# Gate and up projections by seven block products, the down projection as a phase of its own, the final norm in the last block

## What is computed

```python
h = h + mixed @ w_out[l]
u = rmsnorm(h, ln2_g[l])
h = h + (jax.nn.silu(u @ w_ffn_gate[l]) * (u @ w_ffn_up[l])) @ w_ffn_down[l]
# after both layers
return rmsnorm(h, final_norm_g)
```

## Time and profile before

| | us |
|---|---|
| median of three runs | 2712.1 |
| profiled execution, its own time | 2710.6 |
| span of that execution, first to last instruction | 2708.5 |
| gate, up and down part of layer 1 (end of the output projection to the end of the down projection) | 723.8 |
| the same of layer 2 | 720.6 |
| from there to the end of the span | 31.1 |

### The profile page before, as it was taken

One profiled execution on the slowest core, in us unless ns is written; L12 is line 12 of the kernel. 1 busy time (PEld: TensorE's weight loads), 2 busy tenths in 40 slices (PEclk: granted clock), 3 DMA queues, 4 the chain that ended last, 5 costly groups with the idle time before them and its releaser, 6 DMA issues. The chain is left out here.

```text
span 2708.5 us, 32110 instructions
## 1 busy us (share of the span) xinstructions
PE 2622.1 (97%) x13272; PEld 2079.0 (77%) x13272; DVE 1265.8 (47%) x1297; ACT 681.0 (25%) x884; POOL 923.8 (34%) x416
## 2 busy tenths in 40 slices
PE   7999998999999999999999999899999999999997
PEld 5777765678888888888877777567888888888885
DVE  7877368522333333333567753964323333333334
ACT  6344156621000000000234331854110000000002
POOL 2000431155444444444520023122664444444432
PEclk9999999999999999999999999999999999999998
DMA  5010200022111111111210111002121111111102
GB/s 180 24 40 16 54 22 1 20 98 62 55 47 46 46 46 46 46 51 57 70 56 19 38 39 43 1 1 86 48 63 58 58 46 46 54 46 46 46 24 62
DMA packets 198129, 129.59 MB, mean 48 GB/s; under 512 B 29330, under 2 KB 187154, under 8 KB 198035
## 3 DMA queue, kind: packets, MB, share of 16 engines
q1 hardware_dynamic: 198034, 128.25, 15.5%
HBM read 115.65 MB, written 12.58 MB: 47 GB/s over the span
## 5 line engine op out<-in xcount | busy, mean ns | idle before, releaser
L221 PE MATMUL ps<-u_hi,w_hi 128*128 128x512 f32 x2304 | 730.3, 398 | 27.3 <-DVE f L867 13.2
L221 PE MATMUL ps<-u_hi,w_lo 128*128 128x512 f32 x2304 | 713.6, 391 | 0.0
L221 PE MATMUL ps<-u_lo,w_hi 128*128 128x512 f32 x2304 | 713.2, 391 | 0.0
L221 PEld LDWEIGHTS ps<-u_hi,w_hi 128*128 128x128 f32 x2304 | 428.6, 189 | 128.4 <-issue 25.0
L221 PEld LDWEIGHTS ps<-u_hi,w_lo 128*128 128x128 f32 x2304 | 434.5, 189 | 91.8
L221 PEld LDWEIGHTS ps<-u_lo,w_hi 128*128 128x128 f32 x2304 | 434.2, 188 | 91.7
L1820 POOL TENSOR_TENSOR w_hi<-w_raw,ones 128x1024 fp32r<-128x1024 f32 x88 | 166.7, 1894 | 417.0 <-PE ps L221 412.5
L1892 DVE TENSOR_TENSOR h<-ps,h 128x1024 f32<-128x1024 f32 x176 | 211.4, 1219 | 157.4 <-PE ps L221 157.4
L1823 POOL TENSOR_TENSOR w_lo<-w_raw,w_hi 128x1024 fp32r<-128x1024 f32 x88 | 250.7, 2849 | 6.9
L1877 DVE TENSOR_TENSOR hidden<-ps,hidden 128x1024 f32<-128x1024 f32 x44 | 53.9, 1224 | 422.1 <-PE ps L221 422.1
L204 POOL TENSOR_TENSOR w_hi<-w_raw,ones 128x1024 fp32r<-128x1024 f32 (+1 forms) x37 | 71.0, 1918 | 481.8 <-DMA w_raw<-w_in 229.6
(11 more groups left out here) (316 smaller groups left out, 2999.8 us busy)
## 6 DMA issues: line engine op xcount, KB each, us to landing
w_raw<-w_gate SPq DMA_DIRECT2D x44, 512.0 KB, 3.7
w_raw<-w_up SPq DMA_DIRECT2D x44, 512.0 KB, 3.8
down_raw<-w_down SPq DMA_DIRECT2D x44, 512.0 KB, 4.8
w_raw<-w_in SPq DMA_DIRECT2D x42, 512.0 KB, 3.9
h_spill<-h SPq DMA_DIRECT2D x16, 512.0 KB, 2.9
w_raw<-w_out SPq DMA_DIRECT2D x16, 512.0 KB, 3.9
h<-h_spill SPq DMA_DIRECT2D x16, 512.0 KB, 7.1
x_in<-x SPq DMA_DIRECT2D x8, 512.0 KB, 6.7
```

Of the source, the lines that this page charges most:

```text
L221: last = nc.tensor.matmul(ps[:, bank0 + half, :], a, b[:, half * HALF:(half + 1) * HALF], start=(k == order[0] and n == 0), stop=(k == ord ...
```

## The change

For one tile of 128 hidden features, gate and up together are a product of a 2x2 block matrix of weights (gate, up by input features 0 to 511, 512 to 1023) with a 2x2 block matrix of activations (those input features by tokens 0 to 511, 512 to 1023). The change computes it with seven block products (Strassen's scheme in Winograd's form) where eight were done. Each of the seven takes four tiles of input features, three passes and 512 tokens: 12 matmuls. P1 and P6 are accumulated in one bank, P5 and P3 in another, P7 and P4 in a third, P2 has a fourth; two sets of four banks alternate from tile to tile. The four weight sums S1 to S4 are made on VectorE for each tile, the four activation sums T1 to T4 once per layer. ScalarE takes the high parts of the seven weight blocks of a tile, POOL the low parts.

The hidden tile is no longer used at once: it is stored to DRAM (`hidden_dram`) and read back in a down phase of 11 chunks, which starts when all 22 tiles of gate and up are done. `h` is overwritten in place to make room, so it is stored to DRAM tile by tile (`h_spilled`) and loaded again ahead of the down phase. The loops of the block are written out, and setup semaphores are given back.

In the last layer the final norm is done in the same block: gains on ScalarE, transposes of the unscaled tiles, the factor per token as a column, applied by ScalarE and VectorE as they copy out of PSUM. The block `final` is gone.

```diff
+        W_ORDER = ["A11", "A12", "A22", "S3", "S1", "S2", "S4"]
+        W_ORDER0 = ["A11", "A12", "S1", "S2", "S4", "S3", "A22"]
+        S_ORDER = ["S3", "S1", "S2", "S4"]
+        PRODUCTS = dict(P1=("A11", "B11"), P2=("A12", "B21"), P3=("S4", "B22"), P4=("A22", "T4"),
+                        P5=("S1", "T1"), P6=("S2", "T2"), P7=("S3", "T3"))
+        BANK = dict(P1=0, P6=0, P5=1, P3=1, P2=2, P7=3, P4=3)
+        P_ORDER = ["P1", "P7", "P5", "P6", "P2", "P3", "P4"]
+        P_ORDER0 = ["P1", "P5", "P2", "P3", "P7", "P6", "P4"]
...
+            def load_weights(sp, i, t):
+                if i == 0:
+                    sp.wait_ge(slot_split, KT - 3 + t)
+                elif t == 0:
+                    sp.wait_ge(w_lo, 7 * i if i == 1 else 7 * (i - 1) + 3)
+                    sp.wait_ge(s_ready, 4 * i)
...
+            def store_hidden(sp, i):
+                sp.wait_ge(hid_done, i + 1)
+                sp.dma_start(hidden_dram[i * P:(i + 1) * P, :], GA[:, :]).then_inc(hid_stored, 16)
...
+            def pe_product(pe, i, name):
...
+                pe.wait_ge(w_lo, weight_at(i, a))
+                if name == "P6":
+                    pe.wait_ge(p1_copied, i + 1)
+                if name == "P3":
+                    pe.wait_ge(p5_copied, i + 1)
+                if name == "P4":
+                    pe.wait_ge(w_summed, i + 1)
...
+            def dve_c22(dve, i):
+                dve.wait_ge(p_done, product_at(i, "P7"))
+                dve.wait_ge(v_copied, i + 1)
+                nc.vector.tensor_tensor(WT[:, :], ps[:, bank(i, "P7"), :], VC[:, :], ALU.add).then_inc(w_summed, 1)
...
+                nc.vector.tensor_tensor(UP[:, HALF:S], WT[:, :], P5C[:, :], ALU.add).then_inc(up_part, 1)
...
+            def dve_c12(dve, i):
...
+                nc.vector.tensor_tensor(GA[:, HALF:S], ps[:, bank(i, "P3"), :], VC[:, :], ALU.add)\
+                    .then_inc(gate_part, 1)
...
+                nc.vector.tensor_tensor(GA[:, :], GA[:, :], RS[:, :], ALU.mult).then_inc(gate_scaled, 1)
...
+            def dve_c21(dve, i):
+                dve.wait_ge(p_done, product_at(i, "P4"))
+                nc.vector.tensor_tensor(UP[:, 0:HALF], ps[:, bank(i, "P4"), :], VC[:, :], ALU.add)\
+                    .then_inc(up_part, 1)
...
+                nc.vector.tensor_tensor(UP[:, :], UP[:, :], RS[:, :], ALU.mult).then_inc(up_scaled, 1)
...
+                nc.vector.tensor_tensor(GA[:, :], GA[:, :], UP[:, :], ALU.mult).then_inc(hid_done, 1)
...
             # SP
+                    for i in range(1, TILES):
+                        load_weights(sp, i, 0)
+                        load_weights(sp, i, 1)
+                        store_hidden(sp, i - 1)
...
             # POOL
+                    for i in range(1, TILES):
+                        for name in W_ORDER:
+                            pool_weight(pool, i, name)
...
             # ScalarE
+                    for i in range(1, TILES):
+                        act_silu(act, i - 1)
+                        act_p1(act, i)
+                        if i + 1 < TILES:
+                            for name in W_ORDER[0:4]:
+                                act_weight(act, i + 1, name)
+                        act_p5(act, i)
+                        if i + 1 < TILES:
+                            for name in W_ORDER[4:6]:
+                                act_weight(act, i + 1, name)
...
+                        act_v(act, i)
+                        if i + 1 < TILES:
+                            act_weight(act, i + 1, W_ORDER[6])
...
             # VectorE, first tile and then the others
+                    u_part("B21", 3)
+                    dve_sums(dve, 0, S_ORDER0[3:4])
+                    for k in range(4):
+                        u_part("T3 raw", k)
+                        u_part("T2 raw", k)
+                    for k in range(4):
+                        u_part("B22", k)
+                    dve_c11(dve, 0)
+                    for name in ("T4 raw", "T2", "T4"):
+                        for k in range(4):
+                            u_part(name, k)
+                    dve_sums(dve, 1, S_ORDER)
                     dve.wait_ge(rstd_ready, 1)
+                    dve_c22(dve, 0)
+                    dve_c12(dve, 0)
+                    for i in range(1, TILES):
+                        dve_c21(dve, i - 1)
+                        if i + 1 < TILES:
+                            dve_sums(dve, i + 1, S_ORDER)
+                        dve_c22(dve, i)
+                        dve_c11(dve, i)
+                        dve_c12(dve, i)
+                        if i + 1 == TILES:
+                            dve_hidden(dve, 0)
+                    dve_c21(dve, TILES - 1)
```

More of the change, by code:

```diff
@@ new lines, in build @@
+        U_HI = [("B11", 0), ("B11", 1), ("T1", 0), ("B11", 2), ("T1", 1), ("UG", 0), ("B11", 3), ("T1", 2), ("UG", 1),
+                ("B21", 0), ("T1", 3), ("UG", 2), ("B21", 1), ("UG", 3), ("B21", 2), ("B21", 3)] + \
+               [(b, k) for b in ("B22", "T3", "T2", "T4") for k in range(4)]
+        U_HI_AT = {x: n + 1 for n, x in enumerate(U_HI)}
+        U_DVE = [("B11", 0), ("T1 raw", 0), ("B11", 1), ("T1 raw", 1), ("T1", 0), ("B11", 2), ("T1 raw", 2), ("T1", 1),
+                 ("B11", 3), ("T1 raw", 3), ("T1", 2), ("B21", 0), ("T1", 3), ("B21", 1), ("B21", 2), ("B21", 3)] + \
+                [(b, k) for k in range(4) for b in ("T3 raw", "T2 raw")] + \
+                [(b, k) for b in ("B22", "T4 raw", "T2", "T4") for k in range(4)]
@@ new lines, in build @@
+        U_DVE_AT = {x: n + 1 for n, x in enumerate(U_DVE)}
+        DRAW = [raw[t] for t in range(2)]
+        DSET = [[at_r(f"down{s}_{x}{t}", 64 + 16 * s + 8 * n + 4 * t, [P, D], F32R) for n, x in enumerate(("hi", "lo"))
+                 for t in range(2)] for s in range(2)]
+        HRAW = [at_u(f"hidden_back{t}", 16 + 4 * t, [P, S]) for t in range(2)]
+        HIDH = [at_r(f"hidden_hi{b}", 16 * b, [P, 2, S], F32R) for b in range(2)]
+        HIDL = [at_r(f"hidden_lo{b}", 16 * b + 8, [P, 2, S], F32R) for b in range(2)]
@@ L2077, in _ @@
-                    act_chunk(act, 0, 0, first=True)
-                    with act.Fori(0, (CHUNKS - 1) // 2) as r:
-                        for b in range(2):
-                            act_chunk(act, 2 * r + (b + 1), (b + 1) % 2)
+                        norm_act(act, norm2, m, SQ2, None, None)
+                        at = sum(steps[:m])
+                        for name, k in U_HI[at:at + steps[m]]:
+                            u_part(name, k)
+                    for name in W_ORDER0[0:5]:
+                        act_weight(act, 0, name)
@@ new lines, in _ @@
+                    for name in ("T2", "T4"):
+                        for k in range(4):
+                            u_part(name, k)
+                    act.wait_ge(proj_done, J_OUT + KT + 1)
+                    norm_rs(act, 0, (rs_part, 1))
+                    act.wait_ge(h_spilled, 16 * KT)
+                    for name in W_ORDER[0:3]:
+                        act_weight(act, 1, name)
+                    act_v(act, 0)
+                    for name in W_ORDER[3:7]:
+                        act_weight(act, 1, name)
@@ L2090, in _ @@
+                    act.wait_ge(rstd_ready, 2)
+                    for part in range(2):
+                        for n in range(0, TT, 2):
+                            t = OUT_ORDER[n]
+                            act.wait_ge(tokens_done, TT * part + n + 1)
+                            nc.scalar.activation(OT[:, t, part * HALF:(part + 1) * HALF], ps[:, t, :], ACT.Copy,
+                                                 scale=RST[:, t:t + 1]).then_inc(out_act, 1)
                 @block.vector
@@ new lines, in _ @@
+                        if m == KT - 2:
+                            dve_sums(dve, 0, S_ORDER0[0:3])
+                            u_part("B21", 2)
+                    u_part("B21", 3)
+                    dve_sums(dve, 0, S_ORDER0[3:4])
+                    for k in range(4):
+                        u_part("T3 raw", k)
+                        u_part("T2 raw", k)
+                    for k in range(4):
+                        u_part("B22", k)
+                    dve_c11(dve, 0)
+                    for name in ("T4 raw", "T2", "T4"):
+                        for k in range(4):
+                            u_part(name, k)
@@ new lines, in _ @@
+                        return
+                    dve.wait_ge(rstd_ready, 2)
+                    for part in range(2):
+                        for n in range(1, TT, 2):
+                            t = OUT_ORDER[n]
+                            dve.wait_ge(tokens_done, TT * part + n + 1)
+                            nc.vector.tensor_tensor(OT[:, t, part * HALF:(part + 1) * HALF], ps[:, t, :],
+                                                    RST[:, t:t + 1].broadcast_to([P, HALF]), ALU.mult)\
+                                .then_inc(out_dve, 1)
```

705 lines of the change are left out of this document (460 added, 245 removed).

## The result

| | before | after |
|---|---|---|
| median of six runs each, us | 2712.0 (2710.6 to 2714.2) | 2722.6 (2721.6 to 2724.4) |
| ratio, 95% interval | | 1.0041 (1.0030 to 1.0052) |
| span of the profiled execution | 2708.5 | 2719.7 |
| feed-forward part of layer 1 / 2 | 723.8 / 720.6 | 732.7 / 730.1 |
| from there to the end of the span | 31.1 | 23.2 |

The kernel became 10.6 us slower. The forecast was 2680: the direction is wrong, though the time lies in the range. The feed-forward part after is read from the start of the first block product (632.3 and 1966.4) to the start of the last addition of the down projection (1365.0 and 2696.5).

A forecast was written before the change was run, and what follows sets the result against it. TensorE, busy 97% of the span, was taken as the bound. Per layer -59.8 + 17.2 + 3 + 22 + 4.9 + 1 + 1.6 - 1.5 = -11.6; twice that and -8.5 is -31.7, giving 2680 us, range 2628 to 2725.

The forecast's parts named there:

- the end: From the last addition to the span's end: final norm with transposes and one-column products, 8.5 us gained (4 to 11).
- Part 1: Gate and up matmuls: 84 passes per tile instead of 96 at the old pace, floor 19.04 us, 59.8 us less per layer.
- Part 3: SP's queue in gate and up: store and loads wait for the previous hidden tile; 20.24 us per tile, 22 us per layer.
- the ring: Loop per tile: hidden tile's end, store and next loads (5.9 us), VectorE's work to the next end; 20.24 us in all.
- list of signs: What a trace would show if right: P3 waits about 1.2 us for the copy of P5, period 20.2, down 24 us into tile 21.
- Part 2: Engine work per tile: VectorE 9.5 us, POOL 9, ScalarE 7, all under 19.04, but VectorE and POOL block each other.
- the hold-ups: VectorE instructions with two SBUF operands wait out a full POOL instruction, also at 512 elements: 4.7 us per tile.
- engine part: The ring from first weight sum to the hidden tile's end: 9.5 us of VectorE's own work and 4.7 of hold-ups.
- The first tile: Start of gate and up: P4 starts 34.6 us after P1, 17.2 us lost per layer, plus 3 for the clock.
- part 5: From up to down: 4.9 us lost before down, about 1 for the clock, 1.6 for reloads of h, nothing for hidden loads.
- the second rival: Gate and up: the ring is longer, from 21.1 us per tile the kernel is slower than before; chance 0.18.
- Without hold-ups 15.5: Lower bound of the ring per tile in us, if VectorE is never held up: TensorE sets the pace, 0 lost.

The follow-up runs named there:

- run 1: Against the kernel after, SP issues tile i's two weight loads ahead of the store of hidden tile i-2, so loads no longer wait for the previous hidden tile: 2644.3 us.
- run 4: Against the kernel after, GpSimd fills the low parts of gate and up weights with zero from tile 2 on, reading no operand: 2645.1 us.
- run 2: Against the kernel after, loads still wait for the previous hidden tile's end, but its store goes out behind the two loads: 2681.7 us.
- run 3: Against the kernel after, loads still wait for the previous hidden tile's end, but its store goes out from ScalarE's queue instead of SP's: 2736.0 us.
- run 5: Against the kernel after, down weights and hidden tiles of chunk 1 are issued between the fourth and fifth reloads of h, not behind all eight: 2707.7 us.

## Why the prediction was wrong

Against the sum, per layer, layer 1 / layer 2:

| step | forecast | measured |
|---|---|---|
| gate and up, first to last pass | 462.1 | 475.5 / 477.3 |
| pause ahead of down | 5.9 | 3.6 / 3.5 |
| down phase | 241.0 | 250.3 / 249.1 |
| all of it against before | -11.6 | +8.9 / +9.5 |
| the end | -8.5 | -7.9 |

The forecast of 462.1 is 22 x 19.04 + 17.2 + 3 + 22 and the 1.0 of the norm's sum.

*Right.* Part 1, the pace: 19.04 us per tile in the open ring (run 1). Part 3, the mechanism and place of the ring: P3 waits for the copy of P5, its chain runs hidden, DMA, VectorE, as the forecast's list of signs says. Part 2, the hold-ups at 512 elements: S2 1.65, gate x RS 2.26, gate x up 2.21 in the chain above, and 0.69 for S2 without POOL's subtraction (run 4). The Trainium skill ("SBUF — State Buffer", section Terms) gave that rule, and the traces agree. The engine part is 14.3 us in almost every round, as summed. The first tile, as a whole: P4(0) 32.2 and 33.1 us after P1, forecast 34.6. Down starts 24.6 and 23.6 us into tile 21, forecast 24. The end: 8.5 forecast, 7.9 measured, read from the traces of before and after; no run undid this part alone. The rows of the end in the kernel after, which answer to the earlier trace rows: TensorE's transposes and the first one-column products, then SP's stores.

```profile
2696.29 3.22 PE L2283 MATMUL ps<-constants,final_scaled 128*128 128x128 f32 x28
2699.34 0.28 PE L2295 MATMUL ps<-ones,acc 128*128 128x1 f32 x2
2699.49 0.36 PE L2297 MATMUL ps<-ones,sq 128*128 128x1 f32 x2
...
2706.71 7.60 SPq L2177 DMA_DIRECT2D out<-out_tokens  x8
```

*Wrong in size: the transfers of the ring (part 3).* I took 5.9 us out of 5.3 to 6.9. The median is 6.44, the mean 6.65, with three to five rounds per layer of 6.9 to 7.9, at or above my upper bound of 6.9. I had argued that the store needs only the time in which the load behind it starts up. Run 2 shows that the store ahead costs 1.0 us, and run 3 that another queue doesn't save it. Some 0.45 of it is that the loads are issued later, behind the store. The rest is that they take longer from issue to landing, `w_up` 5.5 us and not 4.9. For `w_gate` it is 4.4 and not 3.7, though its issue takes 0.38 us in one and 0.37 in the other, so there the longer landing isn't slower issue. What in the queue or the DMA engines makes it stays open. The period came to 21.0 and not 20.24. 0.77 x 18 to 19 rounds is 14 us. Cut at the start of tile 1, the first tile lost 17.6 and 18.5 us against 21.2 forecast (17.2 + 3 + 1.0), and the tiles behind it 39.0 and 39.9 against 22: 19 rounds of 1.96, and not 18 of 1.2, are 37.3 of that. In all, gate and up took 13.4 and 15.2 more than forecast. This is the ring of the second rival, which put the turning point at 21.1 us per tile, just above the measured 21.0.

*Wrong: "each chunk's hidden loads are issued a chunk ahead: nothing" (part 5).* It holds for every chunk but chunk 1. I had looked at the eight reloads of `h` and at the bandwidth, and not at the queue position of what stands behind them, nor at VectorE's queue, in which the low parts of chunk 1 stand ahead of half the additions. It costs 9.3 and 8.1 us over the forecast; run 5 gives 8.4 and 7.4 of them back.

*Together.* +13.4 - 2.3 + 9.3 is 20.4 for layer 1, +15.2 - 2.4 + 8.1 is 20.9 for layer 2, against 20.5 and 21.1 from the last but one line of the table. With 0.6 for the end and 0.7 in stretches between, that is the 42.9 us between the forecast's span of 2676.8 and the 2719.7 measured. By these sums either error alone would have left the kernel faster: with the ring as forecast 2694, with the down phase as forecast 2705.

*The bounds.* "Without hold-ups 15.5" was too low: run 4 has 6.4 + 11.8. A bound that only takes a cost away must ask what was waiting under it. In the first tile the parts were off too: I took 13 us of hold-ups and 21 of VectorE's own work, and layer 2 has 9.8 and 22.3, with 0.8 of waiting. That the start of P4(0) came within 1.5 us of the forecast is in part luck, as the two errors have opposite signs.

*Clock.* In the stretch from 2289.7, at whose start P3 ends a wait of 2.9 us, the granted clock is 0.50, the 1.2 GHz level, for 6.8 us. The forecast had only counted this at the first tile and the start of down. In the ring it hardly lengthens the round, since the engine part is 14.6 us there and 14.3 to 14.4 in the others. The slow passes, some 6 us in layer 2, fill what would be waiting: P3 of the next tile doesn't wait at all.

## What to carry to other kernels

When less matrix work makes room, the next bound is often not an engine but a loop through a queue: list, for each instruction that waits in an in-order queue, what stands behind it, go round until you are back, and add the lengths. If the sum is near the pace, open the loop (here by putting the store behind the next loads, 78 us) before tuning anything in it: inside a closed loop a sooner start is worth nothing, and every microsecond costs once per round. Check the first and last rounds of each phase by themselves, since a load that is a chunk ahead in the steady state can stand behind everything else at the seam (here 20 us in the two down phases).

## What the hardware showed that I had not expected

- A 512 KB store that starts with two 512 KB loads delays them by 1.4 us if it comes from another queue at the same moment, and by 1.0 us if it is issued 0.43 us ahead on the same queue (both against a store right behind the loads). Issued right behind them it adds 0.1: the load of `w_up` lands 4.9 us after its issue, and 4.8 in run 1, where no store is near.
- The time SP spends on an issue depends on what is ahead of it. The load of `w_up` takes 0.58 us as the second of a pair (run 3) and 0.99 as the third of a burst that a store leads. In run 2 the store, then third, takes 1.30.
- Taking GpSimd's subtractions away returned 55% of VectorE's hold-ups (2.6 of 4.7 us) in a steady round, where other waits stood under them, and nearly all (6.7 of 7.6 us) in the first tile of layer 2, where VectorE's queue has 0.8 us of waiting.
